# Splitting the fourth query tile by token stream and spreading the second stream's half tiles over the expert slots

## What is computed

```python
h2 = x * (1.0 + scale2) + shift2          # x: after the first layer norm
q = (tb @ w_query).reshape(-1, PEER_HEADS, 2, PEER_HALF_DIM)      # 1024 x 2048 weights
sc = jnp.einsum('thjd,jkd->thjk', q, sub_keys)
val, idx = lax.top_k(sc, PEER_TOPK)       # 16 of 128 keys, twice per head
cand_s = val[:, :, 0, :, None] + val[:, :, 1, None, :]
top_s, pos = lax.top_k(cand_s, PEER_TOPK) # 16 of 256 pairs
eidx = jnp.take_along_axis(cand_i, pos, axis=-1)
g = jax.nn.softmax(top_s, axis=-1)
act = jax.nn.gelu(jnp.einsum('thk,td->thk', expert_u[eidx], tb))
wts = g * act
out = jnp.einsum('thk,thkd->td', wts, expert_v[eidx])
```

## Time and profile before

| | us |
|---|---|
| median of 3 runs | 1854.13 |
| lowest, highest | 1854.03, 1855.14 |
| the profiled execution | 1863.56 |
| its span, first to last instruction | 1861.4 |

### The profile page before, as it was taken

How to read it: one execution, slowest core, us unless ns; L and a number is a source line. 1 busy time by engine, 2 the same in 40 slices (tenths; PEclk the granted TensorE clock), 3 DMA queues, 4 the chain that set the end, 5 groups by cost and what they waited for, 6 DMA issues and landing times.

```text
span 1861.4 us, 31038 instructions
## 1 busy us (share of the span) xinstructions
PE 1686.8 (91%) x12586; PEld 1600.1 (86%) x12586; DVE 915.0 (49%) x2285; ACT 567.5 (30%) x1528; POOL 329.0 (18%) x301
## 2 busy tenths in 40 slices
PE   4999999999979989878898899776799999999998
PEld 4788878888979888877898899776699999989998
DVE  5642375651376566666977754469634210331200
ACT  0111223840243444434564321235513100132000
POOL 0100000000043444444423312126300000020000
PEclk9999999999999999989998999888899999999999
DMA  8963338354198999999999999999877888745784
GB/s 359 376 235 113 114 124 256 120 220 145 49 403 329 421 406 422 420 419 421 406 421 411 420 420 410 421 378 386 317 266 250 325 294 295 252 175 208 271 295 132
DMA packets 85437, 563.19 MB, mean 303 GB/s; under 512 B 8832, under 2 KB 17568, under 8 KB 17968
## 3 DMA queue, kind: packets, MB, share of 16 engines
q0 software_dynamic: 39776, 289.46, 38.2%
q1 hardware_dynamic: 38416, 251.85, 36.4%
q10 hardware_dynamic: 7104, 19.92, 3.4%
HBM read 556.96 MB, written 4.23 MB: 301 GB/s over the span
## 4 chain that ended last, share of the span: by engine, by line
PE 68%; DMA 14%; DVE 7%; ACT 6%; issue 4%; POOL 0%; another core or an unknown queue 0%; ACTq 0%; SPq 0%; DVEq 0%; POOLq 0%
PE PS L966 30%; PE PS L657 18%; PE PS L945 8%; DMA V<-in_peer_uv_dram,SCR 4%; DMA AUX<-in_peer_uv_dram,SCR 4%; DMA ring<-in_stream_dram 3%; DMA CONV<-in_peer_uv_dram,SCR 3%; DVE PROJ L2207 2%; PE PS L728 1%; PE PS L861 1%; PE PS L894 1%; PE PS L703 1%; PE PS L679 1%; ACT PROJ L1521 1%; ACT L1506 1%
## 5 line engine op out<-in xcount | busy, mean ns | idle before, releaser
L945 PE MATMUL PS<-PROJ,AUX 128*128 128x128 f32 x1712 | 228.3, 294 | 63.9 <-ACT PROJ L1521 63.8
L945 PEld LDWEIGHTS PS<-PROJ,AUX 128*128 128x128 f32 x1712 | 217.2, 207 | 71.4 <-ACT PROJ L1521 71.0
L657 PE MATMUL PS<-H,ring 128*128 128x256 f32 x1184 | 267.6, 387 | 4.2 <-DMA ring<-in_stream_dram 4.2
L966 PE MATMUL PS<-H,ring 128*128 128x128 f32 x2272 | 261.8, 276 | 4.0 <-DMA ring<-in_stream_dram 2.2
L966 PEld LDWEIGHTS PS<-H,ring 128*128 128x128 f32 x2272 | 258.1, 193 | 5.1 <-issue 4.2
L657 PEld LDWEIGHTS PS<-H,ring 128*128 128x128 f32 x1184 | 228.8, 195 | 37.4 <-issue 5.7
L1304 POOL DMA_INDIRECT AUX<-in_peer_uv_dram,SCR x124 | 140.1, 1130 | 479.6 <-PE PS L945 251.1
L945 PE MATMUL PS<-PROJ,CONV 128*128 128x128 f32 x1248 | 166.8, 294 | 38.9 <-ACT PROJ L1521 38.9
L945 PEld LDWEIGHTS PS<-PROJ,CONV 128*128 128x128 f32 x1248 | 160.0, 209 | 42.3 <-ACT PROJ L1521 42.1
L966 PE MATMUL PS<-PROJ,ring 128*128 128x128 f32 x1664 | 191.4, 275 | 3.7 <-DMA ring<-in_stream_dram 3.7
L966 PEld LDWEIGHTS PS<-PROJ,ring 128*128 128x128 f32 x1664 | 188.6, 192 | 4.8 <-DMA ring<-in_stream_dram 4.4
(11 more groups left out here) (351 smaller groups left out, 2043.2 us busy)
## 6 DMA issues: line engine op xcount, KB each, us to landing
ring<-in_stream_dram SPq DMA_DIRECT2D x181, 1024.0 KB
AUX<-in_stream_dram SPq DMA_DIRECT2D x51, 1024.0 KB, 4.8
AUX<-in_ada_dram POOLq DMA_DIRECT2D x16, 1024.0 KB, 9.7
PROJ<-in_ada_dram ACTq DMA_DIRECT2D x4, 1024.0 KB, 20.3
AUX<-in_ada_dram SPq DMA_DIRECT2D x4, 1024.0 KB, 19.9
AUX<-in_stream_dram ACTq DMA_DIRECT2D x4, 1024.0 KB, 8.7
bias_skewed<-AUX ACTq DMA_DIRECT2D x1, 3072.0 KB, 41.8
ring<-in_stream_dram ACTq DMA_DIRECT2D x2, 1024.0 KB
```

Source lines behind the costliest of these rows:

```text
L657: mm = pe.matmul(acc(n, c), w[:, k, c * P:(c + 1) * P], src[:, g * DC + k, :], start=(g == 0 and k == 0 and (c == 0 or groups == 1)), stop ...
L945: mm = pe.matmul(y_chunk(t, c), UV[b][:, D + c * P:D + (c + 1) * P], DIAG[turn % ND], start=(k == 0 and c % 4 == 0), stop=(k == SPT - 1), ...
L966: mm = pe.matmul(acc2(u, n)[:, c * P:(c + 1) * P], w[:, k, c * P:(c + 1) * P], src, start=(g == 0 and k == 0 and (c == 0 or groups == 1)), ...
```

## The change

The fourth query tile (number 3) is split by stream as well, so that four tiles are done in halves and four whole. Stream one's half of tile 3 comes after slot 14 (scores after 16). Stream two's halves of tiles 0, 1, 2 and 3 come after slots 24, 38, 54 and 70; they were after 11, 18 and 24, with tile 3 whole after slot 15. The whole tiles 4 to 7 come after slots 30, 46, 62 and 78 (before: 30, 44, 60, 76). Stream two's norm moves from slots 5 to 10 to slots 12 to 21, and the transposes of stream two's hidden rows from slot 28 to slot 90. The rotation of PSUM banks follows. The number of matmul instructions changes only by tile 3: twice 16 of 128 columns in place of 16 of 256.

```diff
--- before.py
+++ after.py
@@ -55,7 +55,7 @@
           ("rec_in", 1, 8), ("rec_out", 1, 4), ("up0", 1, 16), ("down0", 4, 4),
           ("att_in", 1, 7), ("uk_uv", 1, 1), ("att_out", 1, 4), ("up1", 1, 16), ("down1", 4, 4)]
 TILE0, COLT0 = {}, {}
-SPLIT = 3
+SPLIT = 4
 
 
 def _number_tiles():
@@ -171,9 +171,10 @@
     jobs += [("xs", i) for i in range(8)] + [("cb", g) for g in range(GROUPS)]
     jobs += [("gn", g) for g in range(GROUPS)]
     jobs += [("m1", 0), ("v1", 0), ("qh", 0, 0), ("h2", 0), ("h2", 1), ("sh", 0, 0), ("qh", 1, 0), ("sh", 1, 0)]
-    jobs += [("m1", 1), ("qh", 2, 0), ("sh", 2, 0), ("v1", 1), ("qh", 0, 1), ("sh", 0, 1), ("sc", 6), ("sc", 7)]
-    jobs += [("qh", 1, 1), ("sh", 1, 1), ("qh", 2, 1), ("sh", 2, 1), ("h2", 2), ("h2", 3)]
-    jobs += [("sc", c) for c in range(8, 16)]
+    jobs += [("m1", 1), ("qh", 2, 0), ("sh", 2, 0), ("qh", 3, 0), ("sh", 3, 0), ("v1", 1)]
+    for t in range(4):
+        jobs += [("qh", t, 1), ("sh", t, 1), ("sc", 8 + 2 * t), ("sc", 9 + 2 * t)]
+    jobs += [("h2", 2), ("h2", 3)]
     jobs += [("mean", 0), ("var", 0), ("mix0", 0)] + [("rg", 0, c) for c in range(4)] + [("mlp0", 0), ("mix1", 0)]
     jobs += [("wi", 0), ("kv", 0), ("ctok", 0), ("dot", 0, 0), ("dot", 0, 1)] + [("ql", 0, q) for q in range(4)]
     jobs += [("lg", 0, b) for b in range(4)]
@@ -227,8 +228,8 @@
 GATE_TILES = (2, 5, 8, 11, 13)
 
 
-HALF_AT = {4: (2, 0), 11: (0, 1), 18: (1, 1), 24: (2, 1)}
-QUERY_AT = {15: 3, 30: 4, 44: 5, 60: 6, 76: 7}
+HALF_AT = {4: (2, 0), 14: (3, 0), 24: (0, 1), 38: (1, 1), 54: (2, 1), 70: (3, 1)}
+QUERY_AT = {30: 4, 46: 5, 62: 6, 78: 7}
 OUT_TILES = 4
 OUT_HOMES = (0, 1, 2, 6)
 
@@ -1102,9 +1103,9 @@
                     half_query(*HALF_AT[n])
                 if n - 2 in HALF_AT:
                     half_scores(*HALF_AT[n - 2])
-                if n == 7:
+                if n == 17:
                     variance(1)
-                if n == 28:
+                if n == 90:
                     hidden_rows(2)
                     hidden_rows(3)
                 if n in QUERY_AT:
@@ -1659,13 +1660,13 @@
                     half_score_out(*HALF_AT[n - 3])
                 if n == 4:
                     gate_exp(1)
-                if n == 5:
+                if n == 12:
                     norm_squares(1)
-                if n == 8:
+                if n == 18:
                     norm_root(1)
-                if n == 10:
+                if n == 21:
                     gained(1)
-                if n == 29:
+                if n == 91:
                     hidden_rows_out(2)
                     hidden_rows_out(3)
                 if 40 <= n < 48:
@@ -2422,9 +2423,9 @@
                     pick_pairs(1)
                 if n == 3:
                     pick_experts(1)
-                if n == 5:
+                if n == 12:
                     center(1)
-                if n == 9:
+                if n == 20:
                     normed_chunks(1)
                 if j + 2 < TT * HEADS:
                     if k == (3 if j else 8):
```

## The result

The changed kernel is **slower**: 1867.1 us median of 4 runs (1862.13 to 1870.67) beside 1854.64 us (1854.03 to 1855.95) for the kernel before, a ratio of 1.0057 with an interval of 1.0043 to 1.0072. By the ratio that is about 10.5 us more (the medians, of four runs each, lie 12.5 apart) where 6 us less were forecast, and it lies outside the range given.

A forecast was written before the change was run, and what follows sets the result against it. The slots were taken as bound by the gathers' bytes, so only idle DMA time could be won: 11.4 us lost before less 5.3 after gives 6.1 us, 1854.1 - 6.1 = 1848.0 us, range 1842.5 to 1854.5.

The forecast's parts named there:

- the walk: Slot-by-slot reckoning of how late each value ends after the change; greatest lateness 5.3 us, at slot 32.
- the yardstick: Slot n's value must end by 529.7 + 2.49 n us, plus 2.49 per weight tile loaded; greatest lateness is DMA time lost.
- Its test on before: In the kernel before, slot 16's value came out 11.8 us late, where the windows gave 11.4 us lost.
- the 11.4 us to be won: Idle DMA time in the kernel before, 550 to 600 us, at 325 GB/s instead of 421.
- the sign given for it: VectorE's wait before head 3's keys would be under 6 us if the forecast was right.
- Slots 14 to 32: Part following lateness after the change: 2.5 us at value 15, 4.4 at value 25, 5.3 at value 32.
- Stalls I can't see: Three open costs: TensorE's clock 0 to 1.3 us, tile 4's load 0 to 1, the 670 to 690 us dip -1.7 to 0.
- The slower rival: Tiles 4 to 7 arrive late; TensorE waits 12.6 us at tile 4; 6.5 us slower, 1860.6 us; chance 0.12.
- The clock's price: TensorE's slower clock after waits at slots 9 and 22, 0 to 1.3 us added, taken as 0.
- The thin cover: Slots 38 to 78: only 1.9 us spare per 16 slots; dips cut the gain to 2.7 us, 1851.4 us; chance 0.20.
- The value of slot 31 ending near 614.5 us: Sign that the forecast was right: slot 31's value ends near 614.5 us instead of 625, 5.1 us late.
- The rule weighed: ScalarE's table switch for the norm's root: 1.28 us each from the rows; the skill's 2.66 would raise the forecast 0.4 us.

## Why the prediction was wrong

**What bounds the kernel: right.** The slots stay bound by the gathers' bytes (421 and 418 GB/s where nothing waits), and what they lose goes to the end: behind them TensorE is busy 497 of 513 us, as in the earlier trace rows. In the trace after, slot 30's value is 1.8 us later than the line without loads, slot 32's is 16.6, of which one load's 2.49 are free: 14.1 late, where the walk said 5.3. By slot 48 it is about 17 late, two loads counted, beside 18.4 us lost by the windows, so the yardstick held within 2 us. Its test on before left out tile 4's load, issued at 569.02: with it slot 16 is 9.3 us late, and the 11.7 that fit the windows stand at slot 19. And the 11.4 us to be won were those of one trace; the second trace of before loses 9.5 in all its slots, the first 13.1, the dip of 1.7 with it.

**Slots 4 to 30: right.** Value 25 was forecast 4.4 late and is 4.8 (6.5 in the second trace). Between slots 9 and 24 TensorE's longest wait is 2.70 us, under the 3 named. VectorE's wait for head 3's scores went from 13.41 to 7.40 us, not to 4, outside the sign given for it.

```profile
568.06 0.49 DVE L2142 MAX8 SCR<-PROJ 128x8 f32<-128x128 f32 x2 [7.40 <-ACT PROJ L1486]
```

**The step that failed is the end of "Slots 14 to 32".** It charged tile 4 with 6.9 us and its scores, and nothing else. Of the 8.8 us missing, 8.1 are the four costs shown above. They fall under two heads.

*Seen and priced too low, in "Stalls I can't see":* tile 4's load, 0 to 1 us, taken as 0. It was wanted 7.3 us after its issue and was there 2.9 us later than that. The price came from tile 5 of before, whose bytes had come within 7 to 8.5 us of its place coming free; with a need at 7.4 us that is already no margin, and 10.2 us were measured to the first matmul (9.4 to 10.4 in the seven traces in which TensorE waited for it). The slower rival had the mechanism right and the point of decision too far out: it asked for a landing of over 13.5 us, because it charged only the wait. The wait also brought half clock to part of the tile itself (1.76 us more), which its sum left out. The clock's price, 0 to 1.3 us, I had tied to waits at slots 9 to 22 alone.

*Not seen:* `gate_exp`. I priced the norm's root with its two table loads, but took the order of ScalarE around slots 31 and 47 as unchanged. It is unchanged; what changed is that a whole tile now stands ahead of it at slot 46 too, and that TensorE arrives there late. Worse, the wait of about 2 us behind the tiles was in the trace that the prediction read (TensorE at slot 32, columns as above):

```profile
628.16 2.05 PE L945 MATMUL PS<-PROJ,AUX 128*128 128x128 f32 x16 [2.09 <-ACT PROJ L1521]
```

I passed it over because it cost nothing: slots 16 to 19 had set the loss at 11.8. When I let slot 16's lateness go, the sum should have asked of each later wait whether it was now in front. The runs show the size: with the switch under the tile, 10 to 11 us come back; in the kernel before, while slots 16 to 19 led, the same step was worth 2.4 us, with nothing and 4.3 at the interval's ends.

**The thin cover: real, small.** The dip after slot 46 is there (330 GB/s), as that rival's sign said; but it is ScalarE's table switch that makes it: with the switch under the tile, 650 to 680 us move 421 GB/s. The halves' own work is worth 1 to 2 us (with the halves cut, 1.0045 for 1.0051). The rival gave 1851.4 us, a smaller gain and no loss.

**One sign misled.** "The value of slot 31 ending near 614.5 us" came true: it ends at 613.05 + 1.79 = 614.8. But the first gather was issued at 505.10 in this trace and at 509.77 in that of before. Counted from it, the value is 10.1 us late (the line is at 505.10 + 19.9 + 31 x 2.49 + 2.49 = 604.7 us), not 5.1. A sign in absolute time says nothing where the start moves by 4.7 us from one execution to the next.

**The rule weighed.** The rows of after show ScalarE's two switches around `gate_exp` from 613.92 to 616.84, 2.92 us with the exponential between. The Trainium skill (ScalarE: Activation LUTs, What ACT_TABLE_LOAD costs) counts about 2.66 us for each; that makes an estimate of 5.3, and the trace doesn't agree. The Trainium skill (DMA: Bandwidth & Descriptors, Queues, rings and completion order) also says that the queues take turns on each engine. That the trace agrees with: SyncE's queue had 33 to 50 per cent of the engines while gathers were queued. But sharing in turns doesn't make a load early: at that share 1.05 MB takes 5 to 7.5 us, and that is after 2 us to the first byte (issued at 594.15, none up to 596).

**What stays open.** The traces place 6.5 to 9 of the 10.5 us. Two ways to 0.997 were run, one of them with few moves (the split and the switch); whether moving the halves or the norm as well has any worth of its own isn't settled, and neither is what the norm's move cost in the changed kernel (1.0042 with the norm back, 1.0051 without).

## What to carry to other kernels

When a change takes away the wait that sets the loss, go through all later waits that cost nothing so far and price each in full, with the state in which its engine then arrives: here two waits of 2 to 3 us, one of them coming again behind later tiles, with the slower clock behind them, made a loss of 10 us of an order that gains 5 without them. Put a table switch, or any fixed cost of a helper engine, into the time in which that engine stands waiting for a long job, ahead of the instruction that waits, not behind it. And give a load that is freed late the landing time measured at full traffic (10 us here for 1 MB) before its user stands in the order.

## What the runs showed of the hardware

- **The clock makes a short wait dearer.** TensorE had been busy without a break from 581.12 us on; behind 2.89 us of waiting, the 32 matmuls of the tile took 8.83 us for 7.07, and behind 2.08 us more, 16 of the values' 3.30 for 1.95, with a granted clock of 0.83 and 0.91 in those windows and 0.50 from 605 to 608 us, 1.2 GHz for 2.4. In five more traces a tile behind 2.00 to 3.09 us of waiting took 8.83 us, and one behind 1.16 us took 7.14. It doesn't follow from one wait's length alone: in the same trace two values behind waits as long took their 2.05 us (below), and with tile 4's load taken away the 2.09 us at slot 32 had no such effect.

```profile
554.93 2.05 PE L946 MATMUL PS<-PROJ,AUX 128*128 128x128 f32 x16 [2.09 <-ACT PROJ L1522]
...
565.04 2.05 PE L946 MATMUL PS<-PROJ,AUX 128*128 128x128 f32 x16 [2.70 <-ACT PROJ L1522]
```

- **A table load of ScalarE is 1.28 us**, with the next activation 0.01 to 0.02 us behind its end in the rows of after above.
- **Single executions scatter by 0.4 per cent** to either side of the median (1848.5 to 1863.0 us for the kernel before), and the first gather's issue alone lies between 504.4 and 509.8 us in these traces.
- **A 1 MB load beside full gather traffic is usable 9.4 to 10.4 us after its issue** (seven traces). In the one of after it had 33 to 50 per cent of the DMA engines' time while its bytes came, at 377 to 401 GB/s in all.
